# Seven block products for seven of the eight weight chunks of a pooled input projection, its result kept in DRAM

## The reference

```python
u = rms_norm(x, norm_in_g)
proj = einsum('bsd,de->bse', u, w_in)                       # 1024 x 4096
pool_x, pool_z, m_x, m_z = split(proj, 4)                   # 1024 features each
# pool_x in four groups of 256: centred mean over 2, 4, 8 or 16 tokens, minus itself, then x pool_w[g]
y_pool = pool_mixer(pool_x, pool_w, pool_scale) * silu(pool_z)
y_m = mlstm_branch(m_x, ...) * silu(m_z)
h = x + concat([y_pool, y_m]) @ w_out
```

## Time and profile before

| | us |
|---|---|
| median of 3 runs (1169.76 to 1170.4) | 1170.21 |
| span of the profiled execution, first to last instruction | 1168.5 |
| PE busy in it | 1158.7 (99%) |
| DVE, POOL, ACT busy | 678.5, 455.9, 359.2 |
| DMA, mean rate | 80 GB/s |

### The profile page before, as it was taken

The page is one execution under the profiler, slowest core; times in us unless marked ns, Lnnn a source line. Parts: engine busy times, 40 slices in busy tenths (PEclk is TensorE's granted clock), DMA queues, the critical chain, the costliest instruction groups (busy, mean ns, idle before and its releaser), DMA issues.

```text
span 1168.5 us, 17252 instructions
## 1 busy us (share of the span) xinstructions
PE 1158.7 (99%) x6599; PEld 946.1 (81%) x6599; DVE 678.5 (58%) x1249; ACT 359.2 (31%) x720; POOL 455.9 (39%) x437
## 2 busy tenths in 40 slices
PE   9999999999999999999999999999999999999997
PEld 6888888888888868888878888878988887777786
DVE  5645557334368502157777883894699434556668
ACT  6312121100012212445665631242111134553322
POOL 2424222223333223354657656304223323455534
PEclk9999999999999999999999999999999999999999
DMA  7321121343312112300113242123121130133113
GB/s 241 109 81 45 36 81 36 123 152 114 109 36 72 64 64 90 101 23 23 50 34 112 88 171 73 72 100 95 40 88 36 37 100 1 38 122 124 39 38 141
DMA packets 75075, 93.56 MB, mean 80 GB/s; under 512 B 13938, under 2 KB 54090, under 8 KB 74483
## 3 DMA queue, kind: packets, MB, share of 16 engines
q1 hardware_dynamic: 67270, 88.73, 22.7%
q10 hardware_dynamic: 7724, 3.74, 1.2%
HBM read 75.11 MB, written 18.92 MB: 80 GB/s over the span
## 4 chain that ended last, share of the span: by engine, by line
PE 93%; DVE 4%; DMA 1%; ACT 1%; issue 1%; POOL 0%; ACTq 0%; DVEq 0%; POOLq 0%
PE bank L918 22%; PE bank L920 22%; PE bank L919 22%; PE bank L1219 4%; PE bank L1194 4%; PE wide L1210 2%; PE wide L1412 2%; PE bank L1158 1%; PE bank L1147 1%; PE bank L1135 1%; PE wide L920 1%; PE wide L919 1%; PE wide L918 1%; PE bank L1387 1%; DVE h L1910 1%; PE wide L1387 1%
## 5 line engine op out<-in xcount | busy, mean ns | idle before, releaser
L687 POOL CAST whi<-wraw 128x2048 fp32r<-128x2048 f32 x31 | 58.8, 1898 | 454.1 <-PE bank L920 404.1
L918 PE MATMUL bank<-u_hi,wlo 128*128 128x512 f32 x488 | 190.4, 390 | 0.0
L920 PE MATMUL bank<-u_hi,whi 128*128 128x512 f32 x488 | 189.9, 389 | 0.0
L919 PE MATMUL bank<-u_lo,whi 128*128 128x512 f32 x488 | 189.9, 389 | 0.0
L689 POOL TENSOR_TENSOR wlo<-wraw,whi 128x2048 fp32r<-128x2048 f32 x32 | 153.1, 4784 | 3.0 <-ACT whi L2488 0.5
L918 PE MATMUL bank<-x_hi,wlo 128*128 128x512 f32 x312 | 123.5, 396 | 0.0
L920 PE MATMUL bank<-x_hi,whi 128*128 128x512 f32 x312 | 121.6, 390 | 0.0
L919 PE MATMUL bank<-x_lo,whi 128*128 128x512 f32 x312 | 121.5, 389 | 0.0
L918 PEld LDWEIGHTS bank<-u_hi,wlo 128*128 128x128 f32 x488 | 91.6, 188 | 19.9 <-POOL wlo L689 0.8
L920 PEld LDWEIGHTS bank<-u_hi,whi 128*128 128x128 f32 x488 | 91.6, 188 | 19.0
L919 PEld LDWEIGHTS bank<-u_lo,whi 128*128 128x128 f32 x488 | 91.6, 188 | 18.9
...
## 6 DMA issues: line engine op xcount, KB each, us to landing
wraw<-in_w_in SPq DMA_DIRECT2D x26, 1024.0 KB, 5.5
wraw<-in_w_out SPq DMA_DIRECT2D x12, 1024.0 KB, 5.1
...
hst<-in_x SPq DMA_DIRECT2D x4, 1024.0 KB, 5.0
hpool<-hst SPq DMA_DIRECT2D x4, 1024.0 KB, 4.1
smz<-mzs SPq DMA_DIRECT2D x16, 256.0 KB, 2.0
h<-hpool SPq DMA_DIRECT2D x4, 1024.0 KB, 7.5
...
```

The source lines that it names most:

```text
L687: g_.tensor_copy(whi[w % 2][:, :, :], wraw[:, :, :]).then_inc(s["w_hi"], 1)
L918: pe.matmul(ps, al, bh, start=(k == 0), stop=False)
L919: pe.matmul(ps, ah, bl, start=False, stop=False)
L920: return pe.matmul(ps, ah, bh, start=False, stop=(k == nk - 1))
```

## The change

- Chunk 0 stays. For chunks 1 to 7 the product of a chunk (2 halves of columns x 2 halves of contraction, times 2 halves of contraction x 2 halves of tokens) is formed from seven block products in place of eight. Each block product is one PSUM bank of 12 matmuls of 128 x 512. A chunk is 84 matmuls in place of 96.
- The data side of the seven is three quarters of u as they are and four combinations `T0` to `T3` of quarters. They are made once: POOL adds high and low part of two quarters (`Tf` 2 and 3), DVE makes six more sums of 128 x 2048, ACT rounds the four into `Thi`, DVE subtracts into `Tlo`. They lie where `xr`, `yp_hi` and `yp_lo` lay.
- The weight side is made for each chunk on POOL (`seven`): four sums or differences of quarters of `wraw`, five roundings and seven subtractions, all of 128 x 512. ACT rounds the first two blocks (`high_block`). `whi` and `wlo` are rings of eight block slots; block b needs product b-8 to be done. `wraw` is loaded in two halves of 512 KB.
- The results are added up on DVE, seven additions of a PSUM bank to a SBUF tile of 128 x 512 per chunk (`add_up`), after one copy on ACT (`keep`); they go to `px` and `sz`.
- The mixing of group g runs inside chunk 2g+2, after its second product; that of group 3 after chunk 7. Its y is stored to DRAM in pieces of 256 KB (`store_y`), and the eight blocks are loaded back in front of the w_out chunks (`load_y`: blocks 0 to 3 in eight loads of 512 KB as `l_ya` and `l_yb`, blocks 4 to 7 in four loads of 1 MB as `l_yc`). `px`'s high part and y's high part use columns of `u_hi` and `u_lo`, so the right halves of four blocks of both are stored to DRAM before (`o_late`, 2 MB) and loaded back (`l_late`) before chunk 12.
- Semaphores are shared with later uses, whose wait values are raised by a constant.

```diff
+SEVEN = range(1, 8)
...
+            def halves(c, f):
+                if c == 1:
+                    sp_.wait_ge(s["w_lo"], 1)
+                else:
+                    sp_.wait_ge(s["w_lo"] if f else s["g_m0"], c if f else c - 1)
...
+            halves(1, 0)
+            halves(1, 1)
...
+            sp_.wait_ge(s["v_ulo"], 12)
+            for part, (u, sl) in enumerate(((u_hi, slice(0, 4)), (u_lo, slice(0, 4)))):
+                sp_.dma_start(late_d[:, part, :, :], u[:, sl, HALF:S].bitcast(F32)).then_inc(s["o_late"], 16)
...
+            def store_y(g):
+                for n in range(4 * g, 4 * g + 4):
+                    j, sl = n // 2, slice(n % 2 * HALF, (n % 2 + 1) * HALF)
+                    sp_.wait_ge(s["v_ylo"], n + 1)
+                    sp_.dma_start(yhi_d[:, j, sl], y_high(n).bitcast(F32)).then_inc(s[f"o_y{n % 2}"], 16)
+                    sp_.dma_start(ylo_d[:, j, sl], yl[:, n % 2, :].bitcast(F32)).then_inc(s[f"o_y{n % 2}"], 16)
+            def load_y(j, sl, name):
+                for place, src in ((yp_hi, yhi_d), (yp_lo, ylo_d)):
+                    sp_.dma_start(place[:, j:j + 2, sl].bitcast(F32), src[:, j:j + 2, sl]).then_inc(s[name], 16)
+            for c in range(2, 8):
+                for f in range(2):
+                    halves(c, f)
+                if c % 2:
+                    g = (c - 3) // 2
+                    store_y(g)
+                    sp_.wait_ge(s["t_mix"], 4 * g + 4)
+                    mix_weights(g + 1)
+            wt(W_OP)
+            left, right, products = slice(0, HALF), slice(HALF, S), 7 * (len(SEVEN) - 1)
+            for i in range(2):
+                sp_.wait_ge(s[f"o_y{i}"], 128)
+            sp_.wait_ge(s["t_prod"], products + 3)
+            load_y(0, left, "l_ya")
+            sp_.wait_ge(s["t_prod"], products + 4)
+            load_y(2, left, "l_ya")
+            load_y(0, right, "l_yb")
+            load_y(2, right, "l_yb")
...
+            wt(W_OP + 1)
+            store_y(3)
+            for i in range(2):
+                sp_.wait_ge(s[f"o_y{i}"], 256)
+            sp_.wait_ge(s["t_prod"], products + 7)
+            load_y(4, slice(0, S), "l_yc")
+            load_y(6, slice(0, S), "l_yc")
...
-            g_.wait_ge(s["v_xn"], NT)
-            for w in range(1, W_MX + 2):
+            g_.wait_ge(s["v_ulo"], 8)
+            for n in range(2):
+                ks = slice(4 * n, 4 * n + 4)
+                g_.tensor_tensor(Tf[:, 2 + n, :, :], u_hi[:, ks, 0:HALF].bitcast(F32), u_lo[:, ks, 0:HALF].bitcast(F32),
+                                 ALU.add).then_inc(s["g_T"], 1)
...
+            def seven(c):
+                b0 = 7 * (c - 1)
+                def low(i, src):
+                    return g_.tensor_tensor(slot(wlo, b0 + i), src, slot(whi, b0 + i).bitcast(F32), ALU.subtract)
+                def part(i, src):
+                    if b0 + i >= 8:
+                        g_.wait_ge(s["t_prod"], b0 + i - 7)
+                    elif b0 + i >= 4:
+                        g_.wait_ge(s["t_gemm"], 4)
+                    step(g_.tensor_copy(slot(whi, b0 + i), src))
+                    return low(i, src)
+                for k in range(2):
+                    g_.wait_ge(s["a_wa"], 2 * c - 1 + k)
+                    low(k, raw(0, k)).then_inc(s["g_blk"], 1)
+                g_.wait_ge(s["l_wraw"], 16 * (c + 1))
+                x = xs[:, :, :]
+                step(g_.tensor_tensor(x, raw(1, 0), raw(1, 1), ALU.add))
+                step(g_.tensor_tensor(raw(1, 0), raw(0, 0), raw(1, 0), ALU.subtract))
+                part(2, x).then_inc(s["g_blk"], 1)
+                g_.wait_ge(s["g_blk"], 6 * (c - 1) + 3)
+                step(g_.tensor_tensor(x, x, raw(0, 0), ALU.subtract))
+                part(3, x).then_inc(s["g_blk"], 1)
+                g_.wait_ge(s["g_blk"], 6 * (c - 1) + 4)
+                g_.tensor_tensor(x, raw(0, 1), x, ALU.subtract).then_inc(s["g_m0"], 1)
+                g_.wait_ge(s["g_m0"], c)
+                part(4, x).then_inc(s["g_blk"], 1)
+                part(5, raw(1, 0)).then_inc(s["g_blk"], 1)
+                part(6, raw(1, 1)).then_inc(s["w_lo"], 1)
+            for c in SEVEN:
+                seven(c)
+            for w in range(W_OP, W_MX + 2):
...
+            def seven(c):
...
+                for i, moving in enumerate(factors):
+                    ps = ring_7(*(("a_part", c), ("v_sum", v0 + 1), ("v_sum", v0 + 6), ("v_sum", v0 + 2),
+                                  ("v_sum", v0 + 4), ("v_sum", v0 + 5), ("v_sum", v0 + 7))[i])
+                    if i < 6:
+                        pe.wait_ge(s["g_blk"], 6 * (c - 1) + i + 1)
+                    else:
+                        pe.wait_ge(s["w_lo"], c + 1)
+                    if c == 1 and i in LATE_T:
+                        pe.wait_ge(s["v_Tlo"], LATE_T[i])
+                    wh, wl = slot(whi, b0 + i), slot(wlo, b0 + i)
+                    for k in range(4):
+                        mm = three(ps[:, :], ((wh[:, k, :], wl[:, k, :]), (moving[0][:, k, :], moving[1][:, k, :])),
+                                   k, 4)
+                    mm.then_inc(s["t_prod"], 1)
+                    if i == 1 and c % 2 == 0:
+                        mix(c // 2 - 1)
+            LATE_T = {2: 1, 3: 2, 5: 3, 6: 4}
+            for c in SEVEN:
+                seven(c)
+            mix(3)
+            pe.wait_ge(s["l_ya"], 64)
...
+                    pe.wait_ge(s["l_yc"], 64)
...
+            def add_up(c, i):
...
+                ps = bank[bank_of[name, 7 * (c - 1) + (1, 2, 6, 4, 5, 6, 7)[i]]]
+                ve.tensor_tensor(dst, ps[:, :], (p1s, p1s, p5s, p1s, p5s, p5s, p5s)[i][:, :], ALU.add
+                                 ).then_inc(s[name], 1)
+            def combine(dst, a, b, op):
+                ve.tensor_tensor(Tf[:, dst, :, :], a, b, op).then_inc(s["v_T"], 1)
+            def whole(dst, k):
+                combine(dst, u_hi[:, 4 * k:4 * k + 4, HALF:S].bitcast(F32), u_lo[:, 4 * k:4 * k + 4, HALF:S].bitcast(F32),
+                        ALU.add)
+            def low_T(i):
+                ve.wait_ge(s["a_T"], i + 1)
+                ve.tensor_tensor(Tlo[:, i, :, :], Tf[:, i, :, :], Thi[:, i, :, :].bitcast(F32), ALU.subtract
+                                 ).then_inc(s["v_Tlo"], 1)
+            ve.wait_ge(s["v_ulo"], 16)
+            whole(0, 0)
+            ve.wait_ge(s["g_T"], 2)
+            combine(0, full(0), full(2), ALU.subtract)
+            whole(1, 1)
+            combine(1, full(1), full(0), ALU.subtract)
+            low_T(0)
+            combine(2, full(1), full(2), ALU.subtract)
+            combine(3, full(3), full(1), ALU.subtract)
+            low_T(1)
...
+            add_up(1, 0)
+            low_T(2)
+            low_T(3)
...
+            def mixed(n):
+                dt, nh = n % 4 // 2, n % 2
+                g = n // 4
+                ps = filled(ve, "t_mix", n + 1, "v_yr", n + 1)
+                if n >= 2:
+                    ve.wait_ge(s[f"o_y{n % 2}"], 32 * (n // 2))
+                ve.wait_ge(s["a_sz"], 2 * g + dt + 1)
+                ve.scalar_tensor_tensor(yr[:, n % 2, :], ps[:, :], VT[:, V_PS + 2 * g + dt:V_PS + 2 * g + dt + 1],
+                                        sz[:, dt, nh * HALF:(nh + 1) * HALF], ALU.mult, ALU.mult
+                                        ).then_inc(s["v_yr"], 1)
+            def low_y(n):
+                ve.wait_ge(s["a_yhi"], n + 1)
+                ve.tensor_tensor(yl[:, n % 2, :], yr[:, n % 2, :], y_high(n).bitcast(F32), ALU.subtract
+                                 ).then_inc(s["v_ylo"], 1)
+            def mixed_all(g, c):
+                n = 4 * g
+                mixed(n)
+                mixed(n + 1)
+                low_y(n)
+                low_y(n + 1)
+                mixed(n + 2)
+                mixed(n + 3)
+                if c:
+                    add_up(c, 0)
+                low_y(n + 2)
+                low_y(n + 3)
+                for i in range(1, 4 if c else 1):
+                    add_up(c, i)
...
+            for k in range(2):
+                high_block(1, k)
+            for i in range(3):
+                pooled(0, i)
+            high_T(0)
+            high_T(1)
+            pooled(0, 3)
+            ac.wait_ge(s["o_late"], 32)
+            high_T(2)
+            high_T(3)
+            keep(1)
+            for c in SEVEN:
+                g = c // 2
+                if c < 7:
+                    high_block(c + 1, 0)
+                if c > 1:
+                    keep(c)
+                if c < 7:
+                    high_block(c + 1, 1)
+                if c % 2 == 0:
+                    for n in range(4):
+                        high_y(4 * (g - 1) + n)
+                    continue
...
```

More of the change, by code:

```diff
@@ L110, in build @@
     first = [0]
-    for _, _, layout in plan:
-        first.append(first[-1] + size[layout])
+    for w, (_, _, layout) in enumerate(plan):
+        first.append(first[-1] + (0 if w in SEVEN else size[layout]))
     NCH = len(plan)
```

(40 more changed lines are left out.)

247 lines of the change are left out of this document (147 added, 100 removed).

## The result

| | before | after |
|---|---|---|
| median of 4 runs each, us | 1170.31 | 1218.86 (1215.41 to 1220.34) |
| ratio, 95% interval | | 1.0414 (1.0398 to 1.043): 48.6 us slower |
| span of the profiled execution, us | 1168.5 | 1218.5 |
| PE matmuls | 6599 | 6515 (84 fewer) |

1232 was forecast; the time lies inside the range and inside the likeliest case's own. The page of the kernel after, against the earlier trace rows: busy times, granted clock in 40 slices, chain that ended last.

The account below looks back on a forecast made before the run. The port pair that DVE and POOL share was taken as bound (84%): 46.2 up to chunk 8 + 7.2 DRAM + 8 clock = 61.4; 1168.5 + 61.4 = 1229.9, plus 1.7: 1232 us. Range 1190 to 1270, likeliest case's own 1198 to 1265.

Parts of the forecast that it names:

- signs of being wrong: In chunks 2 to 7 PE waits rarely, its clock falls for long, or it waits for SP's or ACT's queue, not POOL.
- Matmuls: Chunks 1 to 7: 84 fewer matmuls at 0.2253 us each, -18.9 us.
- The start: POOL's two sums of 128 x 2048 hold up DVE's scaling of x, which PE needs: +6.5 us.
- Chunk 1: DVE's ten operations for T and POOL's 16 take turns; PE waits before blocks 2, 3, 4: 6.7, 7.4, 6.4 us.
- Chunks 2 to 7, POOL as the bound of PE: POOL's and DVE's port work, 160.4 us from 84.7, outlasts PE's 130; with 8.4 for weight loads it ends at 253.5.
- The order on ACT and SP: Queue order holds PE back 3 to 5 us in chunks 2, 4 and 6, but leaves POOL the port: counted as nothing.
- The split of chunk 8: POOL's splitting of chunk 8 may lie in the way of the last mixing: 2.5 us.
- y through DRAM: Loads of y's blocks 4 to 7 end at 290.5, PE's chunk 8 at 283.3: +7.2 us, bounds 0 and 20.
- The clock: PE's waits of 6 to 11 us lower its clock; three block products at 1.2 GHz cost 2.7 more each: +8 us.
- PE stays the bound: Rival: POOL and DVE don't exclude each other, POOL's 18.9 us a chunk fits beside PE: 1157 us, 7%.
- the losses just eat the gain: Rival: port turns less strict, chunks 2 to 7 at PE's pace, start costs half of 27, DRAM 5: 1170 us, 3%.
- The clock never stayed low: Rival it judges: PE at 1.2 GHz from chunk 1 to mixing 3, 94 us in place of 8: 1318 us, 6%.

Follow-up runs that it names:

- both left out: Kernel after without the combinations T and most of each window sum, with y's pieces and weights issued first and chunk 8 split later: 1166.41 us, ratio 0.9964.
- narrow sums: Kernel after with window sums, end corrections and mean minus self over 64 to 78 tokens in place of 1024 to 1055: 1197.47 us, ratio 1.0232.

## Why the prediction was right, and where it missed

The terms of the forecast beside the account, in us. The forecast's waits of chunks 2 to 7 are what its 46.2 leaves: 46.2 - 24.4 + 6 x 2.7 = 38.0.

| | forecast | measured |
|---|---|---|
| matmuls | -18.9 | -18.9 |
| waits at the start | 6.5 | 5.3 |
| waits in chunk 1 | 20.5 | 12.7 |
| waits in chunks 2 to 7 | 38.0 | 5.8 + 3.6 + 10.0 = 19.4 |
| waits for y from DRAM | 7.2 | 3.4 + 9.0 = 12.4 |
| clock | 8 | 19.0 |
| sum | 61.3 | 49.9 |

By the prediction's own signs of being wrong, its mechanism was half right: in chunks 2 to 7 PE does wait rarely, and what it waits for in chunk 2 hangs on SP's and ACT's queues. PE's idling for `wlo` between 40 and 265 us is three waits, all before 76.

**Matmuls.** Right; the accounts of the kernel after and of the one with both left out close with it.

**The start.** As told, with scalings of 4.38 and 4.84; 5.4 came back with the sums moved. (The working's 53.3 for products 0 and 1 doesn't follow from its 47.5, which gives 52.9; nothing hangs on it.)

**Chunk 1.** Right in mechanism and place (before products 2, 3 and 4), too high in size: 5.09 + 4.61 + 3.03. The working took each operation's duration as its time on the port: 3.57 for a turn of both, where the trace has 3.30. By that the low parts of the three blocks were done at 58.4, 67.6 and 75.7 in place of 60.0, 70.1 and 79.2, which is 3.5 of the 7.8 us. The rest is PE's own work at the low clock, which filled time that the forecast has as waiting; so this part of the waits and of the clock is one loss, entered in two rows. Chunk 1 ends at 85.7 in place of 87.4. The Trainium skill states the mechanism (SBUF — State Buffer, "SBUF: two separate sides": VectorE with two SBUF inputs and GpSimd share one port pair, and the one that starts first has it for its whole instruction), and the turns of 3.30 agree with it; the size came from the durations.

**Chunks 2 to 7, POOL as the bound of PE.** This is the step that failed. The forecast was that POOL's and DVE's exclusive work fills the time from 84.7 to 245, and that PE waits for `wlo` throughout. POOL was done at 221.2. PE didn't wait for POOL at all there; POOL's subtractions were mostly undisturbed (tile `wlo`, 86 to 222 us: duration min/median/max):

```profile
L822 POOL TENSOR_TENSOR wlo<-wraw,whi x22: 1280/1304/2355, 99.6 to 219.1; 128x512 fp32r<-128x512 f32 x22
L822 POOL TENSOR_TENSOR wlo<-xs,whi x18: 1267/1296/2190, 90.8 to 213.3; 128x512 fp32r<-128x512 f32 x18
```

From 86 to 222 us POOL is busy for 126.3 us, with 64 two-input operations and 30 casts that alone take some 100. So DVE held it for some 26 us, where the sum had counted 55 of DVE's work. Three parts of what the sum had too much can be named, the first two as estimates. The window sums of group 3 were all counted ahead of POOL's last block; half of them, some 8 us, came behind it (the second block of columns begins at 222.75). Recorded durations overstate the time on the port: 0.27 us in a turn of 3.30, and once 0.26 (DVE's operation ends at 231.76, and POOL's, 4.62 long alone, ends at 236.12, so it began at 231.50). Over some 40 operations of DVE that is about 10 us. And the loads' 8.4 us were 3.9, POOL's waits for `wraw`. 84.7 + 160.4 - 8 - 10 + 3.9 = 231 is still later than 221.2; some 2 us of that are POOL's start (two operations of chunk 2 were done at 85.6), the remaining 8 stay open.

What PE waited for instead was DVE's chain at two points: products of chunk 2g, additions, window sums, low parts, mixing (3.60 and 10.01). With narrow sums both waits went. The exclusion itself was there, but it hit the other engine: DVE's operations for group 2 took 9.9 us more than alone, and the one collision with the split of chunk 8 made up 7.2 of the 10.01 (the split moved). No run takes POOL's turns away from group 2, so that its wait of 3.60 is owed to them is argued from the durations and not shown. The forecast counted this work, but as a share of the port and not as a chain, and so named POOL where DVE was waited for.

**The order on ACT and SP, counted as nothing.** It cost 5.82 in chunk 2 and half of the 5.68 us that PE was busy in the low stretch beside it, 2.8; in chunks 4 and 6 nothing, against "3 to 5 us in chunks 2, 4 and 6". That the order is worth something to POOL was right, with the other one the time grew by 5 us; but what it gives POOL is weights in time and not a free port.

**The split of chunk 8, 2.5.** Right in place: 4.2 us on one short operation (4.87 against 0.69), and 3.4 us of time.

**y through DRAM.** Too low, 7.2 for 12.4. Counted from chunk 8's start, the loads of blocks 4 to 7 were to be asked for 16.5 us later and chunk 9 to start after 29.0; it was 23.7 and 36.1 (272.92 and 285.29, less 249.21). The loads themselves took 12.4 us, and 12.5 were given them. What was missing is the wait of 3.35, a bank held by the store of a piece, which also puts off the last pieces (stored at 267.26). The working's 278 is moreover 2 us above its own terms (261.5 + 10 + 2.5 + 2.0).

**The clock.** Three waits were taken to cost a product at half clock each; nine of the ten did, in the half-clock stretches shown. But this term is worth something mostly in an account: with the clock kept up in six waits, 1.3 us came back of 10.4.

So 26 us too much in chunks 1 to 7 stood against 16 too little for y and the clock. That 1232 came within 14 us is in part luck: the errors had opposite signs, and they are not all independent, since PE's slow work filled waits. The verdict hung on none of it: the work on T alone, 23.9 us, exceeds the gain of 18.9.

**The rivals.** That PE stays the bound holds for single stretches, the longest from 111 to 187 us, and not for the kernel. That the losses just eat the gain didn't come: the start and chunk 1 cost 18.0 of the 27, but DRAM 12.4 in place of 5 and DVE's chain came on top. The clock never stayed low. The range's 5 to 30 for chunks 2 to 7 holds the working's own figure only if it is counted against the kernel before (21.8, measured 11.2); the waits alone are 38.0.
